# Expert stage: first query by halves, gain products and memory units moved, last four rows gathered as halves

## The reference, cut to what matters

```python
def peer_ffn(hn, wq, subkeys, u_tab, v_tab):      # T=256, 8 heads, 2 halves of 128, 128 keys, top 16
    q = (xt @ wq).reshape(T, PEER_HEADS, 2, PEER_HALF)
    s = jnp.einsum('thpd,hpkd->thpk', q, subkeys)
    s1, i1 = lax.top_k(s[:, :, 0], 16);  s2, i2 = lax.top_k(s[:, :, 1], 16)
    cand = s1[..., :, None] + s2[..., None, :]     # 256 candidates
    top_s, pos = lax.top_k(cand, 16)               # 16 of 16384 experts per token and head
    gate = jax.nn.softmax(top_s)
    # for each token, head and k:  act = gelu(x . u_tab[idx]);  out += gate * act * v_tab[idx]
```

## Time and profile before

| | us |
|---|---|
| median of 3 runs | 3317.72 |
| the runs | 3307.78, 3317.72, 3317.82 |
| the profiled execution | 3309.41 |
| its span | 3307.6 |
| PE busy in the span | 2866.0 (87%) |
| DVE busy | 2440.9 (74%) |
| ACT busy | 770.4 (23%) |
| POOL busy | 623.9 (19%) |
| q0 (gathers) | 536.90 MB, 39.3% of 16 engines' span |
| q1 (loads and stores of SP) | 328.24 MB, 31.2% |

### The profile page before, as it was taken

One profiled execution on the slowest core, in us unless ns is written; L12 is line 12 of the kernel. 1 busy time (PEld: TensorE's weight loads), 2 busy tenths in 40 slices (PEclk: granted clock), 3 DMA queues, 4 the chain that ended last, 5 costly groups with the idle time before them and its releaser, 6 DMA issues. The chain is left out here.

```text
span 3307.6 us, 44552 instructions
## 1 busy us (share of the span) xinstructions
PE 2866.0 (87%) x17520; PEld 2250.9 (68%) x17520; DVE 2440.9 (74%) x4649; ACT 770.4 (23%) x1992; POOL 623.9 (19%) x520
## 2 busy tenths in 40 slices
PE   8999977777777889877777777999998999998898
PEld 8889843333333788533333325999887999997798
DVE  7455677777776886777777767878646878777786
ACT  4222212222222343222222222011323001023300
POOL 0000034444444100344444441000000000000000
PEclk9999988888988999988888888999989999999999
DMA  6454599999999635899999996665204666652464
GB/s 206 148 171 153 172 397 421 417 409 421 396 403 421 230 114 188 354 420 412 416 412 408 401 421 253 196 204 160 68 28 148 191 206 182 204 182 87 134 197 148
DMA packets 470274, 868.25 MB, mean 262 GB/s; under 512 B 18864, under 2 KB 398640, under 8 KB 402352
## 3 DMA queue, kind: packets, MB, share of 16 engines
q0 software_dynamic: 73728, 536.90, 39.3%
q1 hardware_dynamic: 396048, 328.24, 31.2%
q10 hardware_dynamic: 288, 0.24, 0.0%
HBM read 855.89 MB, written 9.44 MB: 262 GB/s over the span
## 5 line engine op out<-in xcount | busy, mean ns | idle before, releaser
L2768 PE MATMUL banks<-arena,arena 128*128 128x512 f32 x1744 | 922.3, 688 | 318.5 <-ACT arena L2843 318.1
L2768 PEld LDWEIGHTS banks<-arena,arena 128*128 128x128 f32 x1744 | 373.5, 221 | 848.7 <-issue 458.1
L2726 POOL DMA_INDIRECT arena<-in_peer_uv,arena x512 | 618.9, 1209 | 1320.6 <-PE banks L2768 667.8
L3001 DVE CUSTOM_DVE_ANT_0 arena<-arena,normed 128x1024 f32<-128x1024 f32 x512 | 626.4, 1224 | 241.2 <-DMA arena<-in_peer_uv,arena 238.7
L456 DVE TENSOR_TENSOR weight_ring_part<-weight_ring,weight_high_parts 128x2048 fp32r<-128x2048 f32 (+2 forms) x244 | 539.9, 2213 | 8.4
L3558 PE MATMUL banks<-normed_columns_part,weight_high_parts 128*128 128x256 f32 x1408 | 395.0, 281 | 3.3 <-DVE weight_ring_part L456 2.7
L3559 PE MATMUL banks<-normed_part,weight_high_parts 128*128 128x256 f32 x1408 | 392.8, 279 | 0.0
L3560 PE MATMUL banks<-normed_columns_part,weight_ring_part 128*128 128x256 f32 x1408 | 392.6, 279 | 0.0
L453 DVE CAST weight_high_parts<-weight_ring 128x2048 fp32r<-128x2048 f32 (+2 forms) x244 | 289.8, 1188 | 84.5 <-PE banks L879 60.6
L877 PE MATMUL banks<-weight_high_parts,arena_part 128*128 128x256 f32 x1200 | 335.8, 280 | 11.9 <-PEq L396 9.7
L879 PE MATMUL banks<-weight_high_parts,arena_part 128*128 128x256 f32 x1200 | 333.2, 278 | 0.0
(11 more groups left out here) (599 smaller groups left out, 4272.5 us busy)
## 6 DMA issues: line engine op xcount, KB each, us to landing
weight_ring<-in_ffn_w_gate SPq DMA_DIRECT2D x88, 512.0 KB, 3.7
weight_ring<-in_ffn_w_up SPq DMA_DIRECT2D x88, 512.0 KB, 4.8
weight_ring<-in_ev_w_in SPq DMA_DIRECT2D x33, 1024.0 KB, 5.3
weight_ring<-in_ffn_w_down SPq DMA_DIRECT2D x32, 1024.0 KB, 5.2
weight_ring<-in_od_w_in SPq DMA_DIRECT2D x23, 1024.0 KB, 5.3
weight_ring<-in_xa_wkv SPq DMA_DIRECT2D x16, 1024.0 KB, 5.6
weight_ring<-in_peer_wq SPq DMA_DIRECT2D x16, 1024.0 KB, 34.8
weight_ring<-in_ev_w_out SPq DMA_DIRECT2D x12, 1024.0 KB, 5.4
```

What stands on the lines that cost most here:

```text
L2726: pool.indirect_dma_start(out=ring[:, slot(i, s), :], out_offset=None, in_=table, in_offset=bass.IndirectOffsetOnAxis(ap=index[:, i % 2, s ...
L2768: mm = pe.matmul(k.ps[:, 2 * b + half, :], diag[:, g % 2, s, :], v, start=n == b * PEER_TOPK, stop=n == last_mixed[b])
L3001: dve.tensor_tensor_reduce(out=ring[:, here, 0:D], in0=ring[:, here, 0:D], in1=k.xn[:, i % NB, :], scale=1.0, scalar=0.0, op0=ALU.mult, op ...
```

## The change

- `split_next` is cut in two: `open_split` does the cast (L453) and remembers it. `land` without a post norm opens the split of tile taken+1 ahead of its last `keep_low`.
- `scale_vector` is cut into `mean_vector` and `invert_vector`.
- Head 0: half 0's query is copied by itself and its two scores are taken after the third chunk of half 1. DVE searches half 0, then takes the reciprocal, then half 1. Half 1 uses bank 5, head 1's query bank 0.
- The gain products stand in `search_first` behind the first eight indices. SP's wait for them is unchanged.
- Of the six memory results, four stay ahead of the first mix; the fifth and sixth follow mixes 0 and 1 on PE, and spreads 0 and 1 on ACT.
- All groups are fours. The last four rows are gathered as eight halves (all u, then all v) from a table of half rows, with indices 2i and 2i+1 made by DVE in search 14; v halves have signals of their own, for which PE and DVE wait.
- PE turns block 0 before mix(last) and waits there for its landed sums. SP's last feed waits for the third v half instead of the dots.
- Some semaphores are shared between steps that don't overlap.

The diff, cut to its core:

```diff
+        if self.opened != n:
+            self.open_split(dve, n)
+        dve.wait_ge(self.split.sem, 2 * at + 1)
+        dve.tensor_tensor(low, w, high.bitcast(F32), ALU.subtract).then_inc(self.split.sem, 1)
...
                 if post is None:
+                    if self.splits == self.taken + 1 and self.splits not in self.whole:
+                        self.open_split(dve, self.splits)
                     self.keep_low(dve, tiles - 1, nxt, high_out, low_out)
...
+    cut_rows = total_rows - GROUP
+    groups = [range(a, a + GROUP) for a in range(0, total_rows, GROUP)]
+    ahead = max(len(sides) - 2, 0)
...
-            sp.wait_ge(k.dots.sem, k.dots.start + total_rows - 1)
+            sp.wait_ge(k.down_in[GROUP - 2].sem, k.down_in[GROUP - 2].start + 16)
             k.feed(sp)
...
+            def half_row(pool, n, part):
+                i, s = n // PEER_TOPK, n % PEER_TOPK
+                signal = k.rows_in[slot(i, s)] if part == 0 else k.down_in[n - cut_rows]
+                pool.indirect_dma_start(
+                    out=ring[:, slot(i, s), part * D:(part + 1) * D], out_offset=None, in_=half_table,
...
+                    half_row(pool, n, 0)
+            for n in range(cut_rows, total_rows):
+                half_row(pool, n, 1)
...
+            def first_head():
+                query_part(0, 0, range(KC)).then_inc(k.produced.sem, 1)
+                query_part(0, 1, range(3))
+                pe.wait_ge(k.query_kept.sem, k.query_kept.start + 1)
+                score_part(0, 0, 0)
+                score_part(0, 1, 0).then_inc(k.scored.sem, 1)
+                query_part(0, 1, range(3, KC)).then_inc(k.produced.sem, 1)
+                pe.wait_ge(k.query_kept.sem, k.query_kept.start + 2)
+                score_part(0, 0, 1)
+                score_part(0, 1, 1).then_inc(k.scored.sem, 1)
...
                 pe.wait_ge(k.memory_in.sem, memory_loaded)
-                k.multiply_side(pe, u0, u0 + 4 * extra, bank_at=LATE_BANK)
+                k.multiply_side(pe, u0, u0 + 2 * ahead, bank_at=LATE_BANK)
...
-                mix(g)
-                if g == len(groups) - 3:
+                if g == len(groups) - 1:
                     pe.wait_ge(k.scores_read.sem, k.scores_read.start + HB)
                     pe.wait_ge(k.landed.sem, k.landed.start + tiles)
                     for t in range(tiles):
                         turn_rows(t, 0)
+                mix(g)
+                if ahead + g < len(sides):
+                    k.multiply_side(pe, u0 + 2 * (ahead + g), u0 + 2 * (ahead + g + 1), bank_at=LATE_BANK)
...
+            keep_first(0)
             k.scale_scalar(act, wide=False)
-            keep_query(0)
+            keep_first(1)
             keep_query(1)
             raise_top(0)
-            for s in sides:
+            for s in sides[:ahead]:
                 k.keep_late(act, s, buffers[s - s0])
...
                 spread(g)
+                if ahead + g < len(sides):
+                    k.keep_late(act, sides[ahead + g], buffers[ahead + g])
...
+            def first_half(p):
+                dve.wait_ge(k.scored.sem, k.scored.start + p + 1)
+                step(dve.max(best[:, p, 0:8], score(0, 0, p)))
+                settled()
+                step(dve.max_index(best_at[:, p, 0:8].bitcast(U32), best[:, p, 0:8], score(0, 0, p)))
+                step(dve.match_replace(work[:, p, :], best[:, p, 0:8], score(0, 0, p), TAKEN))
...
                 index_eight(0, 0)
+                dve.wait_ge(k.gain_in.sem, gain_loaded)
+                for b in range(NB):
+                    dve.tensor_tensor(k.xn[:, b, :], k.x[:, b, :], k.gain, ALU.mult).then_inc(k.tile_out.sem, 1)
+                dve.wait_ge(k.norm_scale.sem, k.norm_scale.start + 1)
                 step(dve.match_replace(cwork, top[:, 0, 0:8], cand, TAKEN))
...
-            k.scale_vector(dve, wide=False)
             while k.splits <= first + 1:
                 k.split_next(dve, first + 2)
+            k.mean_vector(dve)
             k.behind(dve, k.landed)
-            for b in range(NB):
-                dve.tensor_tensor(k.xn[:, b, :], k.x[:, b, :], k.gain, ALU.mult).then_inc(k.tile_out.sem, 1)
+            first_half(0)
+            k.invert_vector(dve, wide=False)
+            first_half(1)
             search_first()
             share_top(0)
...
-                if n == groups[g][0] and 0 < g <= len(groups) - 3:
+                if n == groups[g][0] and g:
                     weigh(g - 1)
-                if g >= len(groups) - 3 and n == groups[g][-1]:
+                if n == total_rows - 1:
                     weigh(g)
```

More of the change, by code:

```diff
@@ L452, in split_next @@
             dve.wait_ge(signal.sem, count)
-        dve.tensor_copy(high, w).then_inc(self.split.sem, 1)
-        dve.wait_ge(self.split.sem, 2 * at + 1)
-        dve.tensor_tensor(low, w, high.bitcast(F32), ALU.subtract).then_inc(self.split.sem, 1)
+        dve.tensor_copy(self.tile(self.high, at % HIGH, n), self.tile(self.ring, n % RING, n)).then_inc(self.split.sem, 1)
+        self.opened = n
     def split_quarter(self, dve, quarter, last):
@@ L2675, in mixed_before, with query_bank @@
         return n - owned_before[n]
+    def query_bank(h, j):
+        if h == 0:
+            return k.ps[:, 4 + j, 0:T]
+        return k.ps[:, 0 if h == 1 else 4 + h % 2, j * T:(j + 1) * T]
     def score(h, b, p):
+        if h == 0 and p == 1:
+            return k.ps[:, 5, T + b * P:T + (b + 1) * P]
         return k.ps[:, 6 + h % 2, (2 * b + p) * P:(2 * b + p + 1) * P]
@@ L2732, in query @@
             def query(h):
                 if h >= 2:
-                    pe.wait_ge(k.query_kept.sem, k.query_kept.start + h - 1)
-                w_high, w_low = k.weights(pe, queries[h])
+                    pe.wait_ge(k.query_kept.sem, k.query_kept.start + h)
                 for j in range(2):
[L2738 to L2745, removed]
+                    query_part(h, j, range(KC)).then_inc(k.produced.sem, 1)
@@ L2747, in scores, with score_part @@
+            def score_part(h, b, p):
+                return pe.matmul(score(h, b, p), qT[:, h % 2, p, b * P:(b + 1) * P], keys[:, 2 * h + p, :], start=True, stop=True)
             def scores(h):
-                pe.wait_ge(k.query_kept.sem, k.query_kept.start + h + 1)
+                pe.wait_ge(k.query_kept.sem, k.query_kept.start + h + 2)
                 if h >= 2:
@@ L2754, in scores @@
                     for p in range(2):
-                        mm = pe.matmul(score(h, b, p), qT[:, h % 2, p, b * P:(b + 1) * P], keys[:, 2 * h + p, :], start=True, stop=True)
+                        mm = score_part(h, b, p)
                 mm.then_inc(k.scored.sem, 1)
+            def first_head():
[8 more added lines that the diff above has]
+                score_part(0, 1, 1).then_inc(k.scored.sem, 1)
             def mix(g):
@@ L2772, in _ @@
             pe.wait_ge(k.fetched.sem, k.fetched.total)
-            for h in range(2):
-                query(h)
-                scores(h)
+            first_head()
+            query(1)
+            scores(1)
             if extra:
                 pe.wait_ge(k.memory_in.sem, memory_loaded)
-                k.multiply_side(pe, u0, u0 + 4 * extra, bank_at=LATE_BANK)
+                k.multiply_side(pe, u0, u0 + 2 * ahead, bank_at=LATE_BANK)
             def turn_rows(t, b):
@@ L2964, in index_eight, with index_halves @@
                                          ALU.mult, ALU.add).then_inc(k.indexed.sem, 1)
+            def first_half(p):
[4 more added lines that the diff above has]
+                step(dve.match_replace(work[:, p, :], best[:, p, 0:8], score(0, 0, p), TAKEN))
+                settled()
+                step(dve.max(best[:, p, 8:16], work[:, p, :]))
+                settled()
+                last = dve.max_index(best_at[:, p, 8:16].bitcast(U32), best[:, p, 8:16], work[:, p, :])
+                if p == 0:
+                    step(last)
+                else:
+                    last.then_inc(k.scores_read.sem, 1)
+            def index_halves():
+                dve.wait_ge(k.indexed.sem, k.indexed.start + HB + 1)
+                rows = index[:, (HB - 1) % 2, PEER_TOPK - GROUP:PEER_TOPK]
+                step(dve.tensor_scalar(halved[:, 0, :].bitcast(U32), rows, 1, None, ALU.logical_shift_left))
+                settled()
+                dve.tensor_scalar(halved[:, 1, :].bitcast(U32), halved[:, 0, :].bitcast(U32), 1, None,
+                                  ALU.bitwise_or).then_inc(k.indexed.sem, 1)
             def search_first():
-                for part in range(4):
-                    find_halves(0, part)
+                settled()
                 find_pairs(0, 0)
```

71 lines of the change are left out of this document (52 added, 19 removed).

## The result

| | before | after |
|---|---|---|
| median of 7 runs each, us | 3317.72 | 3327.59 |
| ratio | | 1.0038 (95%: 1.0025 to 1.0051) |
| profiled execution, us | 3309.41 | 3325.61 |
| its span, us | 3307.6 | 3323.4 |

The account below looks back on a forecast made before the run. It took transfers to bound the two expert stages; per stage +6.2 + 1.0 - 0.8 = +6.4, two stages +12.8 us, so 3330 on the runs' median scale, range 3307 to 3344 (the forecast's own 3319 to 3340).

Parts of the forecast that it names:

- signs: Stage start and end: listed issue times, idle stretches, a gather hole at 453 to 458, last gather packets some 6 us later.
- The total of 12.8: Whole kernel: the summed loss over two expert stages, +12.8 us.
- The 6.2 us: Each stage's start: 6.2 us more without DMA traffic, as the kept memory waits for the moved products; carried to stage end.
- moving two results out is "worth nothing": First mix: moving 32 PE records (7 us) behind it only pays back most of the late start; mix at 449.6 against 447.31.
- Price 0 for the third query tile: VectorE at row 6: the tile lands near 457 in a gather hole, 2 to 3 us wait, cost 0, bounds 0 and +4.
- 6.4: Each expert stage: forecast loss in us, +6.2 + 1.0 - 0.8.
- Rival 2: Row 6: third query tile really late, VectorE stands 14 us, gathers run out; 7 us more, 3337; chance 0.13.
- The end: Stage end: halves and groups of four save 0.8 us per stage, PE's two rows at 1.88 each; bounds -1.7 and +2.2.
- Rival 1: Stage: row 0's 2.2 us lead counts, late loads fill holes at query products; -6.0 to -10, 3308 to 3312; chance 0.34.
- Rival 3: Stage end: four more half gathers each pay a fixed 2.3 us in series, 9.2 a stage, 3348; chance 0.03.
- the later hole (+1.0): First later query product: no load left to fill its gather hole, +1.0 us per stage, bounds 0 and 2.5.

Follow-up runs that it names:

- two tiles first: Changed kernel, products still late, with SyncE issuing the third memory tile and third query tile ahead of its wait for the products: 3324.32 us, ratio 1.0029.
- products early: Changed kernel with only the two gain products put back early, between the reciprocal and the second half search: 3313.52 us, ratio 0.9994 of before.
- all six results ahead: Changed kernel with all six memory results ahead of the first mix, as in the kernel before: 3337.05 us, ratio 1.0076.
- four results behind: Changed kernel with only two memory results ahead of the first mix, the other four behind mixes 0 to 3: 3353.46 us, ratio 1.0128.
- both edits together: Changed kernel with third memory and query tiles issued ahead of the products wait, and four memory results behind mixes 0 to 3: 3315.68 us, ratio 1.0011.
- the two variants of the kernel before: Kernel before with only the gain products moved late, 3337.02 us (1.0062); kernel before with only later query products cut in two, 3307.27 us (0.9974).

## Why the prediction was right, point by point

**Right.** GpSimd's first issue at 420.42 (420.5 forecast), SyncE's kept-memory issue at 422.43 (422.7), no traffic until 422.9 (422.9), PE idle from 422 to 431.5 (430.4), the queue of gathers dry from 454 to 460 while the loads' queue moved 2.27 MB (453 to 458), the third query tile split at 457.02 (landing near 457). These are steps that the prediction named as its signs. One more sign was off: the last gather packets come about 8 us later from the stage's start, not 6, since the halves end about 2 us later than whole rows. The total of 12.8 met the 12.6 of the ratio, and part of that is luck: by the two profiled executions the loss is 16.2, and the terms below miss in both directions.

**The 6.2 us.** The byte deficit is 5.7 and is carried, as forecast. But "as the rest of the stage is transfer bound, I carry the 6.2 to its end" is not the whole of it. The second stage bears it out: with two tiles first the bytes come back and the stage with them, though the wait at row 6 goes at the same time, and the two are not told apart. In the first stage, with two tiles first, the idle stretch is largely used and the stage ends no earlier. That the late first mix, delayed by the same wait, holds it there fits the traces, but no run isolates it. What is shown is that the loss belongs to the products' late place, by "products early".

**Too small: moving two results out is "worth nothing".** The step put it against the old first mix. Beside late products it is worth 5.1 and 6.4 us a stage, 12.6 in the time, since with all six results ahead PE also waits 4.63 us for the third memory tile. The first mix itself came 1.6 later than forecast (451.23 against 449.6): the kept memory landed a microsecond later and 64 records took 17.01 instead of 16.

**Price 0 for the third query tile.** Right in the first stage (0.82 us of idle time, 2 to 3 forecast), wrong in the second: 6.21 us of idle time on VectorE, where the gathers' hole was 3 us instead of 6. That this wait makes the stage's 9.0 out of 6.4 is not shown. The byte deficit does rise by 3 us behind it, but it is back at 6.5 at 360 us and rises to 9.7 only afterwards, without a cause that these runs show. Rival 2 had the mechanism of the wait; its size there was under half of its 14, and it struck one stage here. With four results behind it struck both, for 18 and 19.

**The end.** Forecast 0.8 a stage, measured 1.2 and 0.0 against whole rows. PE has two rows behind the last diagonals, 3.70 us in both stages, as the step had it with 1.88 a row. VectorE's saved waits outweigh that in the first stage and only balance it in the second, where the wait for the fourth row from the end didn't exist.

**The rivals.** Rival 1 (the lead counts, late loads fill the holes) is refuted for this kernel: the lead of 2.3 us was gone by row 1. Rival 3 as well: the halves issue 1.24 us apart, no 2.3 us each, and 9.2 us a stage are nowhere in the times; what the halves do cost is a slower queue, 343 GB/s against 421. By the Trainium skill, "DMA: Bandwidth & Descriptors", section "Anatomy of one DMA — SWDGE (gpsimd) path", each would bear a fixed part of about 2.0 us; the trace, four more issues and an end no later, doesn't show it in series. A rise of the deficit like the later hole (+1.0) is there in the byte count, 6.2 to 7.5 between 60 and 130 us, and was mostly given back by 360 us.

**Open.** Four things are open: what holds the first stage when two tiles go first, where the second stage loses its last 3 us, why both edits together are 8.6 us faster than tiles alone, and the 1.3 us behind the second stage. Of this last, the two variants of the kernel before lag 2.3 and 4.4 us there in their own single executions, so it may be no more than that scatter.

## What to carry to other kernels

Before an operation is moved to let one transfer start sooner, read who else waits for it: here a load's issue stood behind it, and the idle DMA time at the start of a transfer-bound stage didn't come back by its end. A stage with a ring of buffers may start under two bounds, bytes and the first release of a slot, and an experiment that mends one of them alone may then show little; try them together before a cause is dropped. A load with small packets beside a queue of large ones landed in the holes of the other here, so a fix that closes the holes can starve it.

## What the runs showed of the hardware

Late loads cost more the better the gathers run: the third query tile kept VectorE waiting 0.82 us where the gathers' queue was dry for 6 us beforehand, 6.21 us where it was dry for 3, and 17.79 us where it moved 0.7 MB in every 2 us until 463. The halves, in 4 KB packets, moved 343 and 376 GB/s at the ends of the two stages, where whole rows, in 8 KB packets, moved 421 and 426; how much of that is the packets' size and how much GpSimd's issue of 0.5 MB each 1.24 us or more isn't separated. And cutting a matmul sequence of 48 in two or four pieces cost nothing visible in the times, 3305.59 and 3304.36 against 3313.52, although PE then works on them in shorter stretches.
